# Two output projections and one input projection issued as pairs of 512 and 256 columns

## The chip, the cores and the metric

The kernel runs on one core of a Trainium2 chip. Its time is the device time of one execution in microseconds (us). Times below are of single executions; the median is over the runs named.

## The reference

One sequence of T = 256 tokens of width D = 2048 in float32 goes through two transformer-like layers. Cut to what matters here:

```python
# layer 1
h = rms_norm(x, mix_norm)
proj = h @ w_in                       # mixers and gates
merged = sigmoid(g_a)*(y_a @ wb_a) + sigmoid(g_b)*(y_b @ wb_b) + sigmoid(g_c)*(y_c @ wb_c)
x = x + merged @ w_out                # output projection of layer 1
x = x + conv_ffn(rms_norm(x, ffn_norm), w_up, conv_w, conv_b, w_down)
x = rms_norm(x, final_norm)
# layer 2
h = rms_norm_2(x, g_mix)
proj = h @ w_in_2                     # second input projection: latents, rope key, q, k, v, gates
x = x + (g0 * y_a + g1 * y_b) @ w_o_2 # output projection of layer 2
gt, up = split(rms_norm_2(x, g_ffn) @ w_gate_up)
x = x + (silu(gt) * up) @ w_down_2
```

## The kernel before

**Layout.** Activations are kept transposed: a tile has 128 features on the partitions and 256 tokens along the row, and KT = 16 such tiles make a width of 2048. xT is the residual stream, hT the normalised input, and a large arena holds all else. Weights stream from HBM in units: one unit (2048 columns, 1 MB) holds the 16 weight tiles of 128 x 128 that make one output tile. They land in a ring of RING = 4 slots, issued by the SyncE queue as soon as `consumed[s]` says that TensorE is done with the slot.

**High and low halves.** Large projections run in float32r with both operands split: ScalarE rounds a unit to w_high (line 1029), VectorE makes w_low = w - w_high (the helper at line 1459) in place in the ring, AHEAD = 2 units before they are used. Activations are split in the same way. A product of two numbers is high x high + high x low + low x high.

**Two ways to issue it.** `project_split` has three matmuls of 256 columns for each weight tile, all into one half of a bank: w_high with the high activations, w_high with the low ones, w_low with the high ones. `project_pairs` has two: w_high with the high and low activations side by side, 512 columns into both halves of the bank (high sum in half 0, low sum in half 1), and w_low with the high activations, 256 columns into half 0. Whoever drains the bank must then add its halves. Before the change the up projections use `project_pairs` and the down projections the same pattern (`acts_both`, whose high and low tiles lie 44 tiles apart); the output projections and the second input projection use `project_split`.

**Banks.** Unit n of a projection writes bank s = n mod 4; `drained[s]` says when it may be written again. Banks 4 to 7 serve the normalisations and the down projections.

**Output projections** (`merged_out`, once in each layer, 16 units): the drain is in `residual_raw` on VectorE, which adds the bank to xT[:, n]; ScalarE then rounds the new tile with its gain and squares it (`round_raw`), VectorE makes its low part (`lower_raw`) and adds up the squares (`sum_raw`). When the 16 units are done, `drained_all` makes TensorE wait for every drain, and the up projection follows on the raw residual tiles (`ups`: 8 of them in hT as up_early, 8 in the arena as up_late).

**Second input projection.** Its feature-major part has IN2 = 26 units: the first by `raw_unit`, one more, then two and four rounds of four. The input is the raw residual of layer 1 (`in2_high`, `in2_low`: 8 tiles in hT, 8 in the arena, high and low side by side in each), and the norms are put on as a factor when the bank is drained: `P2[:, u] = bank * xrs`. xrs is ready only after a chain that starts behind the first unit: a matmul of ones sums the squares, VectorE and ScalarE take two reciprocal roots with steps of refinement, and units of weights are rounded and lowered in between. After the 26 units come the units that produce tokens on the partitions (`tokens`), which wait for the drains of two banks.

In VectorE's code `link` makes an instruction's successor wait for it, and `tt` is a tensor-tensor operation; nearly all of VectorE's rows have line 1459, that of `tt`. All matmuls have line 486.

Of the kernel before, what the change touches and what calls it, by code (L numbers as in the profile page):

```python
# [36 lines left out]
P = 128  # L37
T = 256
TB = T // P
D = 2048  # L40
KT = D // P
# [139 lines left out]
def build(nc, t, out):  # L181

    with ExitStack() as ctx:
        def sb(name, shape, dt=F32):
            return ctx.enter_context(nc.sbuf_tensor(name, shape, dt))

        def alias(name, base, shape, at=0):

            return nc.alloc_sbuf_tensor_at(name, shape, R32, offset=base + at * T * 4)
# [3 lines left out]
        xT = sb("xT", [P, KT, T])  # L193
# [15 lines left out]
        xrs = sb("xrs", [P, T])  # L209
        xtmp = sb("xtmp", [P, T])  # L210
        ARENA = nc.sbuf_bytes_remaining // 4 // 16 * 16
        arena = sb("arena", [P, ARENA])
        arena_base = nc.sbuf_base - ARENA * 4

        def tiles(at, n):
            assert at + n * T <= ARENA, (at + n * T, ARENA)
            return arena[:, at:at + n * T].rearrange("p (k t) -> p k t", t=T)
# [9 lines left out]
        in2 = [part[:, k] for part, n in ((in2_early, 8), (in2_mid, 3), (in2_next, 1), (in2_late, KT - LATE))  # L227
               for k in range(n)]
        in2_high, in2_low = [x[:, 0] for x in in2], [x[:, 1] for x in in2]
        out_high, out_low = (alias(f"out_{n}", arena_base, [P, KT, T], a) for n, a in (("high", 28), ("low", 46)))  # L230
        out2_high, out2_low = (alias(f"out2_{n}", arena_base, [P, KT, T], a) for n, a in (("high", 18), ("low", 34)))
        y_high, y_low = alias("y_high", arena_base, [P, 12, T], 4), alias("y_low", arena_base, [P, M_TILES, T], 0)
        u_high = alias("u_high", hT_base, [P, S5_TILES, T])
        y2_high, y2_low = alias("y2_high", arena_base, [P, KT, T], 66), alias("y2_low", arena_base, [P, 26, T], 0)
# [38 lines left out]
        P2 = tiles(0, 26)  # L273
# [14 lines left out]
        bank = [ctx.enter_context(nc.psum_tensor(f"bank{i}", [P, 2, T], F32)) for i in range(8)]  # L288
        bank_row = [b[:].rearrange("p a t -> p (a t)") for b in bank]

        def sem(name):
            return ctx.enter_context(nc.semaphore(name))
# [5 lines left out]
        drained = [sem(f"bank_drained{s}") for s in range(RING)]  # L298
# [9 lines left out]
        norm_mean, norm_rooted, norm_done = sem("norm_mean"), sem("norm_rooted"), sem("norm_done")  # L308
# [169 lines left out]
        def _(pe):  # L478
            units = Units(landed, rounded, lowered, consumed, drained)
# [3 lines left out]
            norm = [0]  # L483
# [17 lines left out]
            def unit_split(body, bank_used=True):  # L501
                s, _, _, _, free = units.next(split=True)
                pe.wait_ge(lowered[s], units.lowered[s].value())
                if bank_used and (not isinstance(free, int) or free > 0):
                    pe.wait_ge(drained[s], free)
                body(s).then_inc(consumed[s], 1)
# [8 lines left out]
            def rounds_split(n, body):  # L515
                with pe.Fori(0, n) as i:
                    units.enter(i, split=1)
                    for j in range(RING):
                        unit_split(body)
                units.leave(n)  # L520

            def mm3(o, s, c, high, low, first, last):

                c = slice(c * P, (c + 1) * P)
                mm(o, w_high[:, s, c], high, first, False)
                mm(o, w_high[:, s, c], low, False, False)
                return mm(o, w_low[:, s, c], high, False, last)

            def each(x):
                return [x[:, k] for k in range(KT)]  # L530
# [13 lines left out]
            def project_split(high, low, waits=None, at=0):  # L544
                def body(s):
                    for k in range(KT):
                        if waits:
                            waits(k)
                        last = mm3(bank[at + s][:, 0], s, k, high[k], low[k], k == 0, k == KT - 1)
                    return last  # L550
                return body

            merges = [0]

            def merged_out(high, low):

                n = merges[0]
                merges[0] += 1

                def waits(k):  # L560
                    pe.wait_ge(merged_lowered, KT * n + k + 1)
                unit_split(project_split(high, low, waits))
                for j in range(3):
                    unit_split(project_split(high, low))
                rounds_split(3, project_split(high, low))

            def project(s):
                for k in range(KT):
                    last = mm(bank[s][:, 0], ring[:, s, k * P:(k + 1) * P], hT[:, k], k == 0, k == KT - 1)
                return last  # L570
# [19 lines left out]
            def drained_all():  # L590
                for s, n in units.all_drained():
                    pe.wait_ge(s, n)
# [3 lines left out]
            def raw_unit(project, second=False):  # L596

                n = raws[0]
                raws[0] += 1

                def waits(k):
                    pe.wait_ge(raw_lowered, KT * n + k + 1)
                unit_split(project(waits))
                pe.wait_ge(raw_summed, (KT - 1) * raws[0])
                mm(bank[4][:, 0], ones[:], xms[:]).then_inc(norm_summed, 1)
                norm[0] += 1
                if second:
                    pe.wait_ge(raw_summed2, KT - 1)
                    mm(bank[5][:, 0], ones[:], sum2).then_inc(norm_summed, 1)
                    norm[0] += 1  # L610
# [99 lines left out]
            for part in range(2):  # L710
                s = take()
# [92 lines left out]
            for f in range(S5_TILES):  # L804
                if f % 2 == 0:
                    s = take()
# [15 lines left out]
            s = take()  # L822
# [10 lines left out]
            s = take()  # L833
# [24 lines left out]
            for j in range(3):  # L858
                unit_split(branches(False))
            rounds_split(3, branches(False))  # L860
            merged_out(each(out_high), each(out_low))
            drained_all()
            raw_unit(lambda waits: project_pairs(ups, waits))
            for j in range(3):
# [2 lines left out]
            down(0)  # L867
            for b in range(2):
                pe.wait_ge(down_drained[b], 1 + KT // 2)
            raw_unit(lambda waits: project_split(in2_high, in2_low, waits), second=True)  # L870
            unit_split(project_split(in2_high, in2_low))
            rounds_split(2, project_split(in2_high, in2_low))
            banks_back()
            rows_back()
            turn_factor()
            rounds_split(4, project_split(in2_high, in2_low))
            tokens(False, in2_high, in2_low)
            sum_squares()
            tokens(True, in2_high, in2_low)
# [100 lines left out]
            for j in range(3):  # L980
                unit_split(branches2(False))
            rounds_split(3, branches2(False))
            merged_out(each(out2_high), each(out2_low))
            drained_all()
            raw_unit(lambda waits: project_pairs(ups, waits))
            for j in range(3):
# [456 lines left out]
        def _(dve):  # L1443
            V = nc.vector
            units = Units(landed, rounded, lowered, consumed, drained)
            chain = Count(dve_chain)
            norm = [0]
            M, ADD, SUB, MAX, MIN = ALU.mult, ALU.add, ALU.subtract, ALU.max, ALU.min

            def link(ins):  # L1450
                ins.then_inc(dve_chain, 1)
                chain.add()
                dve.wait_ge(dve_chain, chain.value())
# [4 lines left out]
            def tt(o, a, b, op=M):  # L1458
                return V.tensor_tensor(o, a, b, op)  # L1459
# [195 lines left out]
            for u in range(MIX):  # L1655
# [24 lines left out]
                if u >= MIX - KT:  # L1680
                    k = u - (MIX - KT)
# [165 lines left out]
            s, _, _, there, _ = units.next(False)  # L1847
# [68 lines left out]
            def residual_raw(gain):  # L1916

                for n in range(KT):
                    s, _, _, there, free = units.next()
                    lower_weights(UNIT)  # L1920
                    dve.wait_ge(consumed[s], there)
                    tt(xT[:, n], xT[:, n], bank[s][:, 0], ADD).then_inc(drained[s], 1)
                    if n:
                        lower_raw(n - 1, ups[n - 1][:, 0], ups[n - 1][:, 1], v(gain, n - 1))
                        sum_raw(n - 1)
                    if n == KT - 1:
                        dve.wait_ge(drained[s], free + 1)
                lower_raw(KT - 1, ups[KT - 1][:, 0], ups[KT - 1][:, 1], v(gain, KT - 1))
                sum_raw(KT - 1)
                raws[0] += 1  # L1930
# [65 lines left out]
            pairs, convs, acts = Count(silu_pair), Count(conv_made), Count(acts_rounded)  # L1996
# [91 lines left out]
            refine(xms[:], xrs[:], xtmp[:], to=mix2_rs)  # L2088
            link(tt(xrs[:], final_rs, mix2_rs))
            V.tensor_copy(xtmp[:, 0:1], xrs[:, 0:1]).then_inc(norm_done, 1)  # L2090


            IN2 = 26
            for u in range(IN2):
                while ahead.pos - base < min(IN2, max(u + AHEAD + 1, 5)):
                    lower_weights(UNIT)
                s, _, _, there, _ = units.next()
                dve.wait_ge(consumed[s], there)
                tt(P2[:, u], bank[s][:, 0], xrs[:]).then_inc(drained[s], 1)
                if 6 <= u < 6 + KT:  # L2100
                    k = u - 6
                    stt(xT[:, k], xT[:, k], v("final_norm", k), final_rs).then_inc(x_normed, 1)
# [45 lines left out]
            for half in range(2):  # L2148
                for g in range(2):
                    k = 2 * half + g  # L2150
# [13 lines left out]
            for h in range(2 * HEADS):  # L2164
                e, m = ES[h % 2], small[:, h % 2]
                s = bank[4 + h % 2]
# [225 lines left out]
```

## Time and profile before

| | |
|---|---|
| median of 3 runs | 3117.86 us (3116.12 to 3118.37) |
| the profiled execution | 3121.36 us |
| its span, first to last instruction | 3119.6 us, mean granted TensorE clock 0.994 |
| TensorE matmul busy | 3083.7 us, 99%, 18712 matmuls |
| TensorE weight loads busy | 2746.7 us, 88% |
| VectorE busy | 1812.5 us, 58% |
| ScalarE busy | 1202.8 us, 39% |
| GpSimd busy | 101.8 us, 3% |
| DMA | 530.23 MB, mean 170 GB/s |

The profile comes from one execution. Matmuls overlap in the array, so the duration of one (0.28 us for 256 columns, 0.39 for 512) is not the distance from one to the next; that distance is read from start times, or from a stretch divided by its number of matmuls. A mean granted clock of 1.00 in a stretch is 2.4 GHz, 0.50 is 1.2 GHz.

### The profile page before, as it was taken

What the parts mean: (1) busy time and instruction counts of PE and PEld (TensorE: products, weight loads), DVE (VectorE), ACT (ScalarE), POOL (GpSimd) and SP (SyncE); (2) the same over time, 40 slices, a digit from 0 to 9 for tenths busy, and PEclk for the clock granted to TensorE, in tenths of its full rate; (3) what the DMA queues carried; (4) which work ended last, traced back from release to release, by engine and by line L of the source; (5) the groups of instructions that cost most, each with busy time, mean ns of one, the idle gap of its engine ahead of it and who ended that gap; (6) DMA issues with size and microseconds to landing.
All of it is one profiled execution on the core that took longest, in us unless ns stands there. A gap on an engine that the chain in (4) does not pass through costs nothing.

```text
span 3119.6 us, 47133 instructions
## 1 busy us (share of the span) xinstructions
PE 3083.7 (99%) x18712; PEld 2746.7 (88%) x18712; DVE 1812.5 (58%) x2356; ACT 1202.8 (39%) x1351; POOL 101.8 (3%) x80
## 2 busy tenths in 40 slices
PE   8999999999999999999999999999999999999999
PEld 8898898889998888888889977788999888888888
DVE  6673352867678888875555333322566666665444
ACT  5453102114444444444443312244445444444333
POOL 0000000000000000000000310000000000000000
PEclk9999999999999999999999999899999999999999
DMA  6554332445555555555555543223455555555555
GB/s 225 185 187 155 108 121 95 159 152 188 183 183 190 192 193 190 188 174 192 187 194 183 183 164 108 81 95 123 162 187 189 188 188 189 190 193 172 192 186 183
DMA packets 80147, 530.23 MB, mean 170 GB/s; under 512 B 9152, under 2 KB 9536, under 8 KB 27712
## 3 DMA queue, kind: packets, MB, share of 16 engines
q1 hardware_dynamic: 80064, 529.07, 49.3%
q8 instruction: 59, 0.97, 0.1%
q14 instruction: 24, 0.20, 0.0%
HBM read 526.94 MB, written 2.10 MB: 170 GB/s over the span
## 4 chain that ended last, share of the span: by engine, by line
PE 97%; DVE 1%; ACT 1%; issue 0%; DMA 0%; SPq 0%; ACTq 0%; DVEq 0%
PE bank L486 97%; DVE w_low L1459 0%; ACT w_high L1029 0%; DVE arena L1459 0%; PE bank L963 0%; DVE arena L1456 0%; DMA xT<-in_xT 0%; DVE arena L1489 0%; DVE xrs L1489 0%; DVE acts_both L1459 0%; DVE xtmp L1459 0%; ACT arena L1114 0%; ACT mix_high L1133 0%; DVE xT L1459 0%; ACT L1152 0%
## 5 line engine op out<-in xcount | busy, mean ns | idle before, releaser
L1459 DVE TENSOR_TENSOR w_low<-ring,w_high 128x2048 fp32r<-128x2048 f32 (+1 forms) x440 | 922.8, 2098 | 434.6 <-ACT w_high L1029 430.8
L1029 ACT ACTIVATE w_high<-ring 128x2048 fp32r<-128x2048 f32 (+1 forms) x448 | 787.1, 1758 | 468.6 <-DMA ring<-in_w_down 232.2
L486 PE MATMUL bank<-hT,ring 128*128 128x256 f32 x2560 | 571.7, 384 | 1.2 <-ACT arena L1376 1.2
L486 PEld LDWEIGHTS bank<-hT,ring 128*128 128x128 f32 x2560 | 489.8, 192 | 76.8 <-issue 7.7
L486 PE MATMUL bank<-up_late,w_high 128*128 128x512 f32 x1408 | 496.9, 392 | 0.0
L486 PE MATMUL bank<-up_early,w_high 128*128 128x512 f32 x1408 | 490.6, 390 | 1.3 <-issue 0.8
L486 PE MATMUL bank<-acts_both,w_high 128*128 128x512 f32 x1408 | 488.5, 392 | 1.5 <-DVE arena L1459 1.3
L486 PE MATMUL bank<-acts_both,w_low 128*128 128x256 f32 x1408 | 393.5, 280 | 0.0
L486 PE MATMUL bank<-up_late,w_low 128*128 128x256 f32 x1408 | 393.4, 279 | 0.0
L486 PE MATMUL bank<-up_early,w_low 128*128 128x256 f32 x1408 | 389.8, 277 | 0.0
L486 PEld LDWEIGHTS bank<-acts_both,w_high 128*128 128x128 f32 x1408 | 264.3, 188 | 58.7 <-issue 1.6
L486 PEld LDWEIGHTS bank<-up_early,w_high 128*128 128x128 f32 x1408 | 264.3, 188 | 58.1 <-issue 0.9
L486 PEld LDWEIGHTS bank<-up_late,w_high 128*128 128x128 f32 x1408 | 264.2, 188 | 57.8
L486 PEld LDWEIGHTS bank<-acts_both,w_low 128*128 128x128 f32 x1408 | 267.3, 190 | 0.0
L486 PEld LDWEIGHTS bank<-up_late,w_low 128*128 128x128 f32 x1408 | 266.8, 189 | 0.0
L486 PEld LDWEIGHTS bank<-up_early,w_low 128*128 128x128 f32 x1408 | 264.3, 188 | 0.1
L1300 ACT ACTIVATE xms<-bank 128x256 f32<-128x256 f32 x176 | 67.9, 386 | 453.5 <-PE bank L486 446.0
L1459 DVE TENSOR_TENSOR arena<-arena 128x256 f32<-128x256 f32 (+6 forms) x283 | 202.3, 721 | 29.7 <-DVE arena L1459 8.2
L486 PE MATMUL bank<-mix_high,w_high 128*128 128x256 f32 x544 | 154.5, 284 | 13.6 <-DVE w_low L1459 13.6
L486 PE MATMUL bank<-mix_high,w_low 128*128 128x256 f32 x544 | 154.2, 284 | 0.0
L486 PE MATMUL bank<-mix_low,w_high 128*128 128x256 f32 x544 | 153.8, 283 | 0.0
L486 PE MATMUL bank<-y_low,w_high 128*128 128x256 f32 x512 | 144.5, 282 | 0.0
(277 smaller groups left out, 4016.2 us busy)
## 6 DMA issues: line engine op xcount, KB each, us to landing
ring<-in_w_up SPq DMA_DIRECT2D x176, 1024.0 KB, 4.8
ring<-in_w_down SPq DMA_DIRECT2D x128, 704.0 KB, 4.0
ring<-in_w_in SPq DMA_DIRECT2D x66, 1024.0 KB, 4.8
ring<-in_w_mix SPq DMA_DIRECT2D x62, 1024.0 KB, 4.9
ring<-in_w_gates SPq DMA_DIRECT2D x48, 1024.0 KB, 4.9
ring<-in_w_branch SPq DMA_DIRECT2D x16, 1024.0 KB, 4.8
ring<-in_w_out SPq DMA_DIRECT2D x16, 1024.0 KB, 4.8
ring<-in_w_o SPq DMA_DIRECT2D x16, 1024.0 KB, 4.8
```

The lines of the kernel that those rows point to most:

```text
L486: return nc.tensor.matmul(o, lhsT, rhs, start=first, stop=last)
L1029: A(w_high[:, s, 0:cols], ring[:, s, 0:cols], ACT.Copy).then_inc(rounded[s], 1)
L1300: A(xms[:], bank[s][:, 1], ACT.Copy).then_inc(half_copied, 1)
L1459: return V.tensor_tensor(o, a, b, op)
```

## The change

The 16 units of each output projection and the 26 feature units of the second input projection are issued by `project_pairs` in place of `project_split`. The high and low activations of the output projections become one tensor each (`out_both`, `out2_both`) over the same places in the arena. The drains add the two halves: `residual_raw` adds half 0 and half 1 to xT one after the other, linked; the drain of the input projection multiplies both halves by xrs, gives the bank back, waits for its own semaphore and adds the second product. Ahead of these drains VectorE waits once for the copy that ends the norm's chain, since xtmp, which that copy writes, now takes the second products.

```diff
-        out_high, out_low = (alias(f"out_{n}", arena_base, [P, KT, T], a) for n, a in (("high", 28), ("low", 46)))
-        out2_high, out2_low = (alias(f"out2_{n}", arena_base, [P, KT, T], a) for n, a in (("high", 18), ("low", 34)))
+        out_both = alias("out_both", arena_base, [P, 2, KT + 2, T], 28)
+        out2_both = alias("out2_both", arena_base, [P, 2, KT, T], 18)
+        out_high, out_low, out2_high, out2_low = out_both[:, 0], out_both[:, 1], out2_both[:, 0], out2_both[:, 1]
...
-            def merged_out(high, low):
+            def merged_out(both):
...
-                unit_split(project_split(high, low, waits))
+                pairs = [both[:, :, k] for k in range(KT)]
+                unit_split(project_pairs(pairs, waits))
                 for j in range(3):
-                    unit_split(project_split(high, low))
-                rounds_split(3, project_split(high, low))
+                    unit_split(project_pairs(pairs))
+                rounds_split(3, project_pairs(pairs))
...
-            raw_unit(lambda waits: project_split(in2_high, in2_low, waits), second=True)
-            unit_split(project_split(in2_high, in2_low))
-            rounds_split(2, project_split(in2_high, in2_low))
+            raw_unit(lambda waits: project_pairs(in2, waits), second=True)
+            unit_split(project_pairs(in2))
+            rounds_split(2, project_pairs(in2))
             banks_back()
             rows_back()
             turn_factor()
-            rounds_split(4, project_split(in2_high, in2_low))
+            rounds_split(4, project_pairs(in2))
...
                     dve.wait_ge(consumed[s], there)
-                    tt(xT[:, n], xT[:, n], bank[s][:, 0], ADD).then_inc(drained[s], 1)
+                    link(tt(xT[:, n], xT[:, n], bank[s][:, 0], ADD))
+                    tt(xT[:, n], xT[:, n], bank[s][:, 1], ADD).then_inc(drained[s], 1)
...
             V.tensor_copy(xtmp[:, 0:1], xrs[:, 0:1]).then_inc(norm_done, 1)
+            dve.wait_ge(norm_done, norm[0])
...
                 dve.wait_ge(consumed[s], there)
-                tt(P2[:, u], bank[s][:, 0], xrs[:]).then_inc(drained[s], 1)
+                tt(P2[:, u], bank[s][:, 0], xrs[:])
+                tt(xtmp[:], bank[s][:, 1], xrs[:]).then_inc(drained[s], 1)
+                dve.wait_ge(drained[s], units.drained[s].value())
+                link(tt(P2[:, u], P2[:, u], xtmp[:], ADD))
```

## Rows read from the trace of the kernel before

**Rows 1.** The page: busy time of the engines, and the chain that ended last, by engine.

```profile
PE 3083.7 (99%) x18712; PEld 2746.7 (88%) x18712; DVE 1812.5 (58%) x2356; ACT 1202.8 (39%) x1351; POOL 101.8 (3%) x80
...
PE 97%; DVE 1%; ACT 1%; issue 0%; DMA 0%; SPq 0%; ACTq 0%; DVEq 0%
```

**Rows 2.** Stretches: busy us (matmuls) by engine, granted clock, DMA share, GB/s.

```profile
810.00:885.00 75.00, 75.00 (x639) 75.00 (x638) 45.58 (x55) 35.53 (x42) 0.00 (x0) 1.00 0.55 184
1654.00:1767.00 113.00, 113.00 (x959) 112.85 (x958) 57.67 (x54) 36.64 (x20) 3.96 (x1) 1.00 0.54 186
900.00:1370.00 470.00, 470.00 (x2729) 414.65 (x2728) 406.82 (x561) 218.67 (x250) 30.13 (x34) 1.00 0.55 188
2873.00:3116.00 243.00, 243.00 (x1404) 214.78 (x1403) 116.13 (x94) 86.24 (x64) 0.00 (x0) 1.00 0.55 188
```

**Rows 3.** The timeline of TensorE inside the up projection: start us, us, what.

```profile
1101.67 0.39 PE L486 MATMUL bank<-up_early,w_high 128*128 128x512 f32 x1
...
1102.01 0.39 PE L486 MATMUL bank<-up_early,w_high 128*128 128x512 f32 x1
...
1102.70 0.39 PE L486 MATMUL bank<-up_late,w_high 128*128 128x512 f32 x1
...
1103.05 0.39 PE L486 MATMUL bank<-up_late,w_high 128*128 128x512 f32 x1
```

**Rows 4.** Groups of matmuls: xcount, then busy us, mean ns, idle before.

```profile
L486 PE MATMUL bank<-out_high,w_low 128*128 128x256 f32 x512 | 144.4, 282 | 0.0
...
L486 PE MATMUL bank<-in_early,w_low 128*128 128x256 f32 x208 | 58.9, 283 | 0.0
```

**Rows 5.** The chain of waits in order of time: start us, us, what.

```profile
888.82 0.77 issue
...
1772.95 0.56 issue
...
2384.44 0.43 DVE xT L1459
```

**Rows 6.** The timeline of VectorE, an xT sum of either kind.

```profile
888.86 0.42 DVE L1459 TENSOR_TENSOR xT<-xT,bank 128x256 f32<-128x256 f32 x1 [0.25 <-PE bank L486]
...
1604.73 0.88 DVE L1459 TENSOR_TENSOR xT<-xT,bank 128x256 f32<-128x256 f32 x2 [0.44 <-PE bank L486]
```

**Rows 7.** The timeline of VectorE at the head of the second input projection.

```profile
1628.82 0.42 DVE L2076 TENSOR_SCALAR xms<-bank 128x256 f32<-128x256 f32 x1 [1.09 <-PE bank L486]
...
1646.96 0.15 DVE L2090 COPY xtmp<-xrs 128x1 f32<-128x1 f32 x1
1647.03 1.08 DVE L1459 TENSOR_TENSOR arena<-bank,xrs 128x256 f32<-128x256 f32 x3
1648.02 2.28 DVE L1459 TENSOR_TENSOR w_low<-ring,w_high 128x2048 fp32r<-128x2048 f32 x1
1650.22 0.42 DVE L1459 TENSOR_TENSOR arena<-bank,xrs 128x256 f32<-128x256 f32 x1
1650.56 2.28 DVE L1459 TENSOR_TENSOR w_low<-ring,w_high 128x2048 fp32r<-128x2048 f32 x1
```

**Rows 8.** The timeline of TensorE there, in brackets what ended its idle time.

```profile
1645.91 0.28 PE L486 MATMUL bank<-in_late,w_low 128*128 128x256 f32 x1
1647.59 0.48 PE L486 MATMUL bank<-in_early,w_high 128*128 128x256 f32 x2 [1.40 <-DVE arena L1459]
```

**Rows 9.** Stretches around stops of TensorE, columns as in rows 2.

```profile
1619.70:1622.40 2.70, 0.25 (x2) 0.00 (x0) 2.61 (x3) 0.02 (x1) 0.00 (x0) 1.00 0.72 209
1992.80:1996.00 3.20, 0.36 (x2) 0.00 (x0) 2.72 (x4) 0.00 (x0) 0.00 (x0) 0.60 0.32 133
1996.00:2014.00 18.00, 17.94 (x37) 10.93 (x38) 2.50 (x7) 3.59 (x6) 0.00 (x0) 0.50 0.00 1
2198.00:2200.80 2.80, 0.40 (x4) 0.16 (x2) 0.50 (x1) 2.76 (x3) 0.00 (x0) 1.00 0.62 173
2200.80:2206.00 5.20, 5.19 (x27) 5.03 (x28) 3.60 (x3) 3.87 (x4) 0.00 (x0) 0.67 0.27 112
```

More of the change, by code:

```diff
@@ L860, in _ @@
             rounds_split(3, branches(False))
-            merged_out(each(out_high), each(out_low))
+            merged_out(out_both)
             drained_all()
@@ L982, in _ @@
             rounds_split(3, branches2(False))
-            merged_out(each(out2_high), each(out2_low))
+            merged_out(out2_both)
             drained_all()
```

## Prediction

> **What bounds the kernel now.** I read the page's busy times and its chain of waits first. TensorE is busy for 99% of the span and the chain runs through its matmuls for 97% [rows 1], so a change counts by what it does to the matmul stream and to the few places where TensorE stands still. Then I read the stages as stretches, to see whether the matmuls that are replaced run at a pace of their own or wait for something. In the first layer's output projection TensorE is busy for all of 75.00 us, as it is in the input projection of layer two and in the up and down projections [rows 2]. The reader is to see that no stage named in the change waits for weights, DMA or VectorE; what differs between them is the time per matmul. Last I read the seams: where TensorE waits for a bank to be drained, since the drain is what the change makes longer.
>
> **The price of the two schemes.** The old form issues three matmuls of 256 columns for one tile of 128 weights, the new one a matmul of 512 and one of 256: both stream 768 columns, so only what each matmul costs beside its columns can be saved. Old form: 639 matmuls in 75.00 us are 117.4 ns each and 959 in 113.00 us are 117.8 [rows 2]. Counted over a unit (16 tiles, 48 matmuls) that is 5.63 to 5.66 us; I take 5.65. New form, by a stage that already uses it with every operand in the arena: the down projection has 1404 matmuls in 243.00 us [rows 2], 173.1 ns each, and 32 of them are 5.54 us; since some matmul records at the edges are missing I take 5.55. The up projection, with half of its moving tiles in hT and half in the arena: 2729 in 470.00 us, 172.2 ns, 5.51 us a unit [rows 2]. The matmuls themselves show where that comes from: a pair from up_early (in hT) is followed by the next after 0.34 us, a pair from up_late (in the arena) after 0.35 [rows 3].
>
> **Output projections: two times 16 units.** The count agrees with 512 matmuls of out_high with low weights [rows 4]. Both out_both and out2_both lie wholly in the arena, high and low halves apart, as acts_both does, so the down projection is the nearest row: 32 x (5.65 - 5.55) = 3.2 us gained. Bounds: nothing, if the pairs stream no better there, and 32 x 0.21 = 6.8 us if every pair ran at up_early's 0.34 us (16 x 0.34 = 5.44 a unit). I take 3.2, because every pair from the arena that I see runs at 0.35.
>
> **Input projection of layer two: 26 units.** in_early's 208 matmuls with low weights are 8 tiles of each of 26 units [rows 4]; those 8 lie in hT and the other 8 in the arena, the up projection's mixture. That gives 5.65 - 5.51 = 0.14 us a unit. But the first four units gain nothing by themselves: they fill the four banks, and the fifth waits for the first drain, which waits for the norm factor. TensorE stops after a matmul at 1645.91 and goes on at 1647.59 [rows 8], released by VectorE. So 22 x 0.14 = 3.1 us.
>
> **What that first drain costs.** The factor's chain begins when the matmul of ones behind the first unit is read, at 1628.82 [rows 7], and that comes 0.14 us earlier. From there the chain is VectorE and ScalarE work that the edit leaves alone, up to the copy at 1646.96. Then the edit adds a wait for this copy (it began 0.07 us before the first product; waiting for its 0.15 us and a semaphore gives about 0.12 more) and a second product before the bank is given back: three products take 1.08 us together, so one more is 0.33 [rows 7]. 0.12 + 0.33 - 0.14 = 0.3 us later than before. I add 0.3.
>
> **What queues behind it on VectorE.** Each drain is now two products, a wait for its own semaphore and a linked sum: 0.33 + 0.42 + 0.04 + 0.42 + 0.04 = 1.25 us in place of 0.33. Three of them stand in front of the weights' low part for the sixth unit. They begin at about 1647.0 and end at 1650.8, that low part (2.28 us [rows 7]) ends at 1653.1, and TensorE, back at 1647.9, wants it at 1653.4. So it is hidden with 0.3 us to spare; if the cover is gone it costs some tenths. Later units give VectorE 2.28 + 1.25 and one operation more of about 0.42, 4.0 us of work in 5.51.
>
> **The seams.** Before each up projection TensorE waits for all banks: 0.77 us after the last output unit in layer one, and behind the last xT sum of 0.43 in layer two [rows 5]. One sum takes 0.42 and two linked ones 0.88 [rows 6], so each seam grows by 0.46: 0.92 us for both. The input projection ends in the same way, the token stage waiting 0.56 us for the last product [rows 5]; a second product adds 0.33. ScalarE gets each xT tile 0.46 us later too, and then rounds it, squares it and rounds weights that are wanted a whole unit later. No DMA is added or moved; a weight slot comes free at most 0.14 us sooner per unit, as in the up projection, which streams at 188 GB/s without a wait [rows 2].
>
> **Sum.** -3.2 - 3.1 + 0.3 + 0.92 + 0.33 = -4.75, say -4.7 us. On the profiled execution's 3121.36 us (span 3119.6) that is 3116.7. The runs' median of 3117.86 lies 3.5 us under that execution, so I put the same difference on it: 3113.2 us, 0.15% less.
>
> The page "TensorE: Matmul & The Clock Gate" of the Trainium skill (section "Wait — 56ns, not 53.3ns?") speaks against it: a warm matmul costs its columns at 2.4 GHz and about 2.5 ns more, whatever its size. An estimate by that page: 54 units x 16 fewer matmuls x 2.5 ns = 2.2 us, and with the costs above the change would bring 0.6 us. The trace does not agree, with 11 ns a matmul above the columns.
>
> **The rivals.**
> A: the pairs bring little or nothing in the new places; something else than the count of matmuls (the order in which w_high and w_low alternate, say) made the up and down projections faster. For it: these projections differ from the changed stages in everything else as well. Against it: two stages with different operands both have it. With no gain at all the costs stay: +1.6 us, 3119.4. The page of the Trainium skill named above is a half-way form of it. 14%.
> B: the 0.35 us is not a matter of the arena, and the output projections get up_early's pace: 6.8 in place of 3.2, and the same for the other half of the input tiles (22 x 0.07 = 1.5) at the most; -8.3 us with the first alone, 3109.5. Against it: the down projection, all arena, shows 0.35 throughout. 14%.
> C: the stop before the fifth unit grows from 1.6 us to 2.5 (it begins 0.6 earlier and ends 0.3 later), and the granted clock falls there from 2.4 to 1.2 GHz. After 2.8 us without matmuls at 2198 the next 5.2 us ran at a mean of 0.67, while after as long a stop at 1619.7 the clock stayed at 1.00 [rows 9]. A short stretch like the first costs (1 - 0.67) x 5.2 = 1.7 us: -3.0, 3114.9. 10%.
> D, the other side: the same stop is followed by a long stretch at 1.2 GHz, as the 3.2 us at 1992.8 were by 18 us at 0.50 [rows 9], now in a stage that TensorE bounds. That loses half of some 20 us, 10 us: +5.5, 3123.4, and it makes the kernel slower as soon as the stretch is longer than 9.4 us. Against it: the stop stays shorter than the one at 1992.8, and the matmuls behind it are dense. 4%.
> E: VectorE falls behind at the head of the input projection, if a drain costs 0.1 us more than I put; some tenths, in the main case's range.
>
> **How the numbers follow.** The likeliest case (58%) is the sum: 3113.2, by itself 3111.5 to 3115. Moving from a gain of nothing to B's needs 3109.5 to 3119.4; leaving out most of D and the far ends of A and B gives 3109.4 to 3119.0. About 0.2% (6.2 us) is what a measurement of this kernel can tell from no change. Faster by more than that: B and the lower tail of the main case, 0.23. Slower by more: D, with something for a wait that I have not seen, 0.06. Within: 0.71.
>
> **What would show it.** In the changed profile, right steps look like this: a unit interval of 5.55 us in the output projections (drains of xT 5.55 apart, not 5.65) and 5.51 in the input projection; 16 matmuls fewer in each of 58 units, 928 in all; the seams before the up projections 0.46 us wider; the fifth input unit starting about 2.5 us after the fourth ends, at clock 1.00, and none between it and the sixth. Wrong would be a unit of 5.65 or of 5.44 us in the output projection, a stretch at half clock behind 1647, or TensorE waiting for w_low in the input projection. The half-clock stretches between 1900 and 2210 lie outside the change but may fall otherwise when all before them is 3 us earlier; the three runs' spread of 2.3 us is my measure for that.

## The result and the profile after

The changed kernel took 3130.86 us (median of 6 runs, 3128.07 to 3131.28), the kernel before 3118.18 (median of 6). The ratio is 1.0031, 95% interval 1.0021 to 1.0041: about 0.3% slower, where 0.15% faster was forecast and 3119.0 was the upper end of the range. (The ratio is not the quotient of the two medians, which is 1.0041.) The profiled execution has a span of 3129.5 us, 9.9 more than the profiled one before; both lie above their kernels' medians, which are 12.7 us apart. The account below is one of the 9.9 us.

The page of the changed kernel first, busy times and then the chain by engine, against [rows 1]; under it stretches inside the output and the input projection, and three stretches at half clock, with the columns of [rows 2]:

```profile
PE 3083.2 (99%) x17784; PEld 2707.9 (87%) x17784; DVE 1845.2 (59%) x2440; ACT 1202.7 (38%) x1351; POOL 101.4 (3%) x80
...
PE 91%; DVE 5%; ACT 3%; issue 1%; DMA 0%; SPq 0%; ACTq 0%; DVEq 0%
```

```profile
810.00:885.00 75.00, 75.00 (x434) 66.29 (x434) 48.45 (x64) 34.21 (x39) 0.00 (x0) 1.00 0.56 195
1660.00:1772.00 112.00, 112.00 (x652) 98.67 (x651) 75.54 (x96) 36.73 (x20) 4.22 (x1) 1.00 0.55 187
889.10:895.90 6.80, 3.89 (x12) 3.35 (x13) 5.55 (x8) 3.90 (x4) 0.00 (x0) 0.50 0.21 88
1653.70:1657.10 3.40, 3.40 (x11) 2.92 (x12) 3.23 (x8) 0.68 (x1) 0.00 (x0) 0.50 0.59 246
2391.00:2397.70 6.70, 5.39 (x17) 4.63 (x18) 4.98 (x8) 3.90 (x4) 0.00 (x0) 0.50 0.14 60
```

The matmuls did what the change says: 928 fewer, 172.8 ns each in the output projection (5.53 us a unit), 171.8 in the input projection (5.50). But the chain that ended last, 97% TensorE before, has 8% of VectorE and ScalarE in it now. A stretch of that chain in the first output projection, and its end ("issue" is time in which the engine waited for nothing that the profile shows):

```profile
840.64 1.82 ACT w_high L1031
842.48 2.29 DVE w_low L1461
845.59 0.51 ACT up_early L1082
846.41 1.81 ACT w_high L1031
...
886.35 5.66 issue
```

It goes round: round a unit's weights, make their low part, (drain a bank), round the new tile, round the next unit's weights, 5.77 us a turn (846.41 - 840.64). And it ends in TensorE standing still until 892.01. TensorE's first matmul behind the seam, in both layers:

```profile
892.01 0.77 PE L487 MATMUL bank<-up_early,w_high 128*128 128x512 f32 x1 [5.76 <-issue]
```

```profile
2392.31 0.80 PE L487 MATMUL bank<-up_early,w_high 128*128 128x512 f32 x1 [4.71 <-DVE xT L1461]
```

Where the 9.9 us are, from the start of each stage's first matmul to the next one's (the seam: from the start of the last output matmul to the start of the first up matmul), in us; "forecast" is what my terms gave:

| stretch | before | after | difference | forecast |
|---|---|---|---|---|
| all ahead of the first output projection | 798.21 | 797.33 | -0.87 | 0 |
| output projection's matmuls, each layer | 90.34 | 88.64 | -1.70, twice | -1.6, twice |
| seam to the up projection, layer 1 | 1.05 | 6.04 | +4.99 | +0.46 |
| seam to the up projection, layer 2 | 0.80 | 4.98 | +4.18 | +0.46 |
| up projection, layer 1 | 485.69 | 487.52 | +1.83 | 0 |
| up projection, layer 2 | 487.27 | 489.77 | +2.50 | 0 |
| second input projection, to the token stage | 151.06 | 151.77 | +0.71 | -2.5 |

The rest is within 0.1 us. The sum is +9.9. The first row is untouched code: a stretch of 6.8 us at half clock fell there before, one of 3.4 us after.

### The profile page after: what moved, and what is told of

Its sections match the earlier page's. It is cut to its first block, busy times and chain, and to the rows that moved or that the text cites. A ratio compares the mean times of both kernels' runs of the same rounds, so it can differ in the third digit from the quotient of the medians.

```text
span 3129.5 us, 45372 instructions
## 1 busy us (share of the span) xinstructions
PE 3083.2 (99%) x17784; PEld 2707.9 (87%) x17784; DVE 1845.2 (59%) x2440; ACT 1202.7 (38%) x1351; POOL 101.4 (3%) x80
## 4 chain that ended last, share of the span: by engine, by line
PE 91%; DVE 5%; ACT 3%; issue 1%; DMA 0%; SPq 0%; ACTq 0%; DVEq 0%
PE bank L487 91%; DVE w_low L1461 3%; ACT w_high L1031 2%; DVE xT L1461 1%; DVE arena L1461 0%; ACT up_early L1082 0%; ACT up_late L1082 0%; PE bank L965 0%; DVE arena L1458 0%; ACT xrs L1073 0%; ACT xtmp L1073 0%; DMA xT<-in_xT 0%; DVE arena L1491 0%; DVE xrs L1491 0%; DVE xtmp L1461 0%
## 5 line engine op out<-in xcount | busy, mean ns | idle before, releaser
L487 PE MATMUL bank<-out_both,w_high 128*128 128x512 f32 x512 | 177.6, 392 | 0.0
```

What stands on the lines that cost most here:

```text
L487: return nc.tensor.matmul(o, lhsT, rhs, start=first, stop=last)
```

## The experiments

The theory drawn from this trace: the output projection has a closed loop beside TensorE. On VectorE the code puts the low weights of unit n+2 ahead of the drain of unit n; they wait for ScalarE's w_high of the same unit; ScalarE makes that only after it has rounded and squared tile n-1, and for this it waits for the drain of unit n-1. A turn took 5.31 us before and the second sum (0.46) makes it 5.77, past TensorE. The rivals: the pairs themselves cost in their new places; the half-clock stretches fell by chance; the input projection is at fault. Ten kernels ran, in three groups (e1 to e4, e5 to e8, e9 and e10), each group with runs of the kernel before on the same chip (medians 3121.61, 3121.32 and 3119.12 us).

**e1, a slower drain without pairs.**

```diff
-                    tt(xT[:, n], xT[:, n], bank[s][:, 0], ADD).then_inc(drained[s], 1)
+                    link(stt(xT[:, n], bank[s][:, 0], 0.5, xT[:, n], M, ADD))
+                    stt(xT[:, n], bank[s][:, 0], 0.5, xT[:, n], M, ADD).then_inc(drained[s], 1)
```

> The kernel before, matmuls untouched; only each drain of an output projection is drawn out: the same sum is added to xT in two linked steps of half the bank each (about 0.5 us more VectorE work per unit, the sums' value unchanged). Loop theory (VectorE drain, ScalarE rounding and squaring of the new tile, ScalarE w_high, VectorE w_low, next drain form a closed loop of 5.31 us that the change lengthened to 5.77, past TensorE's 5.53 to 5.65 a unit): drains 5.85 us apart instead of 5.65, TensorE standing 4 to 6 us before each up projection, a stretch at half clock behind it; 9 to 13 us slower than before, 3127 to 3131. Matmul theory (pairs into two bank halves cost more in their new places): nothing here, within 1 us of before but for the seams (about +1). Clock theory (half-clock stretches that fall by chance): at most +2.

Measured: 3132.82 us (5 runs), ratio 1.0039, interval 1.0025 to 1.0053. VectorE's timeline, with no wait for TensorE ahead of a drain, and TensorE's stops at the two seams:

```profile
884.59 0.88 DVE L1456 SCALAR_TENSOR_TENSOR xT<-bank,xT 128x256 f32<-128x256 f32 x2
...
888.15 2.29 DVE L1459 TENSOR_TENSOR w_low<-ring,w_high 128x2048 fp32r<-128x2048 f32 x1 [1.96 <-ACT w_high L1029]
890.36 0.88 DVE L1456 SCALAR_TENSOR_TENSOR xT<-bank,xT 128x256 f32<-128x256 f32 x2
```

```profile
891.55 0.77 PE L486 MATMUL bank<-up_early,w_high 128*128 128x512 f32 x1 [4.19 <-issue]
...
2391.34 0.51 PE L486 MATMUL bank<-up_early,w_high 128*128 128x512 f32 x1 [3.14 <-DVE xT L1456]
```

The drains are 5.77 us apart (not the 5.85 expected: this operation took no longer than a plain sum), TensorE stands for 4.2 us at the first seam and the clock falls behind it; at the second it stands for 3.1 us and the clock stays at 1.00. The median is above the 3127 to 3131 expected. The trace is that of the fastest of the five runs (3128.15), 6.8 us over the span of before: +3.4 and +2.6 at the seams, +1.6 for the half-clock stretch in the first up projection, less 1.5 ahead of the edit. With every matmul as before, the drain alone brings a loss of the same kind and size: the rival of the matmuls is out. What the slower runs of e1 have on top is not shown.

**e2, the changed kernel, draining first.**

```diff
                     s, _, _, there, free = units.next()
-                    lower_weights(UNIT)
                     dve.wait_ge(consumed[s], there)
                     link(tt(xT[:, n], xT[:, n], bank[s][:, 0], ADD))
...
                         sum_raw(n - 1)
+                    lower_weights(UNIT)
```

> The changed kernel with one order turned round in the output projections' drain: VectorE drains unit n first and makes the low weights of unit n+2 after it, so the loop is open. Loop theory: drains 5.53 us apart, the stop before each up projection 1.4 us in place of 6.0 and 5.0, no half-clock stretch behind it; 10 to 13 us faster than the changed kernel, 3117 to 3121 (3113 to 3117 if the input projection's half-clock stretches stay away as well). Matmul theory: the loss is in the matmuls and stays, 3129 to 3132. Clock theory: the stretches would fall anyway, at most 4 us back.

Measured: 3115.64 us (11 runs), ratio 0.9984, interval 0.9975 to 0.9993. VectorE's timeline:

```profile
880.55 0.88 DVE L1461 TENSOR_TENSOR xT<-xT,bank 128x256 f32<-128x256 f32 x2 [1.74 <-PE bank L487]
...
882.08 2.28 DVE L1461 TENSOR_TENSOR w_low<-ring,w_high 128x2048 fp32r<-128x2048 f32 x1
886.10 0.87 DVE L1461 TENSOR_TENSOR xT<-xT,bank 128x256 f32<-128x256 f32 x2 [1.74 <-PE bank L487]
```

The same operations with the same durations, in another order: now VectorE waits 1.74 us for TensorE in each unit, drains are 5.55 apart, the seams are 1.50 and 1.24 us, and the up projections take 485.69 and 487.23 us, as before. The loss was in the order. And the half-clock stretches at the seams go with the long stops: they stand at the stops of 5.76, 4.71 and 4.19 us (five of five, in the changed kernel, e1 and e3), and at none of the seams with a stop of 2.03 us or less; e1's 3.14 us had none.

**e3 and e4, one half of the change each.** e3 has the output projections in pairs alone, e4 the input projection alone; each undoes the other's lines of the diff. Cut to the calls, against the changed kernel:

```diff
 # e3
-            raw_unit(lambda waits: project_pairs(in2, waits), second=True)
+            raw_unit(lambda waits: project_split(in2_high, in2_low, waits), second=True)
 # e4
-                unit_split(project_pairs(pairs, waits))
+                unit_split(project_split(high, low, waits))
```

> Only the two output projections in pairs; the second input projection as before. Loop theory: carries the whole loss, 9 to 11 us over before, 3127 to 3130. Matmul theory with the input projection at fault: no loss here. The rival that the input projection's head (longer stop, half clock) is the main cause: at most +3.

> Only the second input projection in pairs; the output projections as before. By my prediction's terms -2.5 us when the clock stays up (22 units at 0.15 us less, 0.3 and 0.33 given back): 3115 to 3116; with half-clock stretches at its head, 1.6 us each as the changed kernel's trace has two, +0.7: 3119. Loop theory: no more than that, since this drain has no ScalarE rounding behind it. The rival that this part is at fault: 3124 or more.

Measured: e3 3130.82 us (4 runs), ratio 1.0039 (1.0023 to 1.0054), with the seams of the changed kernel, 6.04 and 4.99 us. e4 3122.31 us (10 runs), ratio 1.0000 (0.9991 to 1.0009); four of its executions lie at 3117 us with a mean granted clock of 0.995 and six at 3121.3 to 3124.5 with 0.993 or 0.992, and the profiled one is of the latter, with two stretches at half clock at the head of the input projection. So the output projections carry the loss. That the input projection gains where the clock stays up is not shown by e4: its fastest executions (3117.08) do not lie under the fastest of before (3116.13). The nearest comparison is that of e8 and e10 below.

**e5, the loop cut on ScalarE instead**, in the changed kernel:

```diff
                     A(ups[n][:, 0], xT[:, n], ACT.Copy, scale=v(gain, n)).then_inc(raw_rounded, 1)
+                    if n < KT - 1:
+                        round_weights(UNIT)
                     square_raw(n)
```

(and the call at the head of the loop's body moved ahead of the loop).

> The changed kernel with one order turned round on ScalarE: in the output projections it rounds the next unit's weights before it squares the new xT tile, which takes 0.3 us out of the loop and nothing else. Loop theory: 5.77 - 0.30 = 5.47 us, below TensorE's 5.54, so drains 5.54 apart, the stop before each up projection near 1.5 us as in e2, and 8 to 12 us faster than the changed kernel. Rival (it is VectorE alone that cannot keep up, by its own work of 2.29 + 0.87 + 0.48 + 0.42 us a unit): ScalarE's order changes nothing, 3129 to 3132.

Measured: 3116.18 us (10 runs), ratio 0.9990 (0.9981 to 1.0000). The seams are 1.51 and 1.25 us. Drains in the first layer:

```profile
836.51 0.87 DVE L1463 TENSOR_TENSOR xT<-xT,bank 128x256 f32<-128x256 f32 x2
...
841.98 0.87 DVE L1463 TENSOR_TENSOR xT<-xT,bank 128x256 f32<-128x256 f32 x2
```

The square weighs 0.3 us in the chain, has nothing to do with VectorE, and taking it out of the loop brings all of the loss back: it is the loop, not VectorE's own work. The turn is the one expected, too: the first drain of the layer is 0.9 us late, the next eleven follow at 5.46 to 5.47 us and so catch up with TensorE, and from there on they stand 5.55 apart, TensorE's own pace.

**e6, a drain lengthened to just below TensorE's pace**, in the kernel before:

```diff
-                    tt(xT[:, n], xT[:, n], bank[s][:, 0], ADD).then_inc(drained[s], 1)
+                    link(tt(xT[:, n], xT[:, n], bank[s][:, 0], ADD))
+                    V.tensor_scalar(xT[:, n], xT[:, n], 1.0, None, M).then_inc(drained[s], 1)
```

> The kernel before with a smaller delay in the drain of the output projections than e1: the bank is added as before, and a linked VectorE product by 1.0 (about 0.33 us) stands behind it ahead of the release. Loop theory: 5.31 + 0.33 = 5.64 us, just below the 5.65 of TensorE's three matmuls, so no lag builds up: drains stay 5.65 apart, each seam 0.33 us wider, +0.7 us in all. Rival (any work added to the drain costs in proportion, e1 having cost some 9 us for 0.5 us a unit): +5 to +7 us.

Measured: 3124.34 us (10 runs), ratio 1.0020 (1.0011 to 1.0029), more than expected. The trace has the output projections at 90.34 us as before and the up projections at 485.75 and 487.60, so nothing builds up. But the first seam is 2.31 us, not 1.38. The first drain of layer 1 begins 0.8 us behind its unit's last matmul; before, with a loop of 5.31, that was made up at 0.34 us a unit, and the loop of 5.64 here makes up 0.01. In both layers the loop has one longer turn, 5.97 us (6.10 in the changed kernel and in e1), where ScalarE's square waits for VectorE's first sum of squares; so the second seam is 1.28 and not 1.13, though its first drain is on time. The larger part is in the input projection, +1.4 us with a stretch at half clock at 1622, in code that it doesn't touch. Neither theory had the number; the proportional one fails on the seams. The same trace shows how much room the loop had: 0.33 us more in each turn still kept TensorE's pace.

**e7 to e10, the clock at the head of the input projection.** The traces so far show a pattern. TensorE stands idle ahead of the fifth input unit, as in [rows 8]; the changed kernel, e2, e4 and e5 each have this row (here of the changed kernel):

```profile
1653.55 0.66 PE L487 MATMUL bank<-in_early,w_high 128*128 128x512 f32 x1 [2.21 <-DVE xtmp L1461]
```

and in each a stretch of 3.4 us at half clock stands behind the stop (1653.7, 1646.7, 1649.9 and 1646.4). With 1.40 us idle, before and in e1, e3 and e6, there is none. These are single traces, one for each kernel. e7 is e2 with this in the norm factor's chain on VectorE:

```diff
             V.tensor_scalar(xms[:], bank[4][:, 0], 1.0 / D, EPS, M, ADD).then_inc(norm_mean, 1)
-            lower_weights(UNIT)
             dve.wait_ge(norm_rooted, norm[0])
             refine(xms[:], xrs[:], xtmp[:], to=final_rs)
```

(That unit's low part is made up later, by the loop ahead of the first drain of this stage.)

> e2 (drain first) with one order more turned round, at the head of the second input projection: VectorE no longer makes a unit's low weights between the first mean and the first refinement of the norm factor, so its chain no longer waits for ScalarE's rounding there. If the longer stop ahead of the fifth unit (2.5 us) is what lets the clock fall (it fell in three traces of three with the input projection in pairs, in none of three without): no stop there, no half-clock stretch, 146 us from the first input unit to the token stage in place of 150.3; 3.5 to 4.5 us faster than e2, a ratio of 0.997 to before. If the clock falls by chance alone, only the 2.5 us. If the factor's chain is not what holds the first drain: as e2.

Measured: 3114.74 us (11 runs), ratio 0.9977 (0.9968 to 0.9986). There is no stop ahead of the fifth unit and no stretch behind it. From the first input unit to the token stage it took 147.76 us, 2.5 less than e2 (150.29), not the 4.3 expected, because a stretch stood at the stage's start this time, at the end of the stop between the down projection and it (the profiled execution is the fastest of the eleven, 3109.35):

```profile
1617.70:1621.10 3.40, 3.29 (x10) 2.84 (x11) 1.48 (x5) 3.34 (x5) 0.00 (x0) 0.50 0.57 239
```

e8 has this last edit alone, on the kernel before.

> The kernel before with that second order alone, all three projections still in threes of 256 columns: what of e7 belongs to the order and not to the pairs. Only the stop of 1.56 us can go, the clock did not fall there: 1.5 us faster, 149.5 us from the first input unit to the token stage in place of 151.06, within 0.1% of before. If more comes back, the factor's chain held more than the stop that the trace shows.

e8: 3118.78 us (10 runs), ratio 0.9999 (0.9990 to 1.0009), 149.42 us for the stage: 1.64 less, as expected.

e9 draws the stop out, on the kernel before:

```diff
             link(tt(xrs[:], final_rs, mix2_rs))
+            for _ in range(2):
+                link(V.tensor_scalar(xrs[:], xrs[:], 1.0, None, M))
```

> The kernel before (all in threes) with the stop ahead of the fifth input unit drawn out from 1.56 to about 2.2 us: two linked VectorE products by 1.0 (0.33 us each) at the end of the norm factor's chain. If it is the length of the stop that lets the clock fall, a half-clock stretch now stands behind 1647 in this trace too, as in the four traces with pairs in the input projection (stops of 2.2 to 2.5 us): +0.7 for the stop and about +1.6 for the clock from the first input unit to the token stage, 153.4 us in place of 151.06. If the stretch belongs to the pairs: +0.7 alone, 151.7, clock 1.00 there.

e9: 3122.43 us (10 runs), ratio 1.0006 (0.9996 to 1.0015). TensorE's row and a stretch behind it:

```profile
1646.26 0.47 PE L486 MATMUL bank<-in_early,w_high 128*128 128x256 f32 x2 [2.06 <-DVE arena L1459]
```

```profile
1647.00:1650.00 3.00, 3.00 (x19) 3.00 (x18) 3.00 (x3) 0.89 (x1) 0.00 (x0) 0.61 0.49 205
```

The clock fell there in this kernel of threes too, once its stop was 2.06 us and not 1.40: pairs are not needed for it. The profiled execution is the slowest of the ten (3126.85), and the interval of the ratio includes 1, so this shows that the clock can fall there, not how often it does. The stage took 154.78 us and not 153.4, because the clock fell at its start as well.

e10 is e7 with the last down bank drained before the next low weights are made:

```diff
+                        last_unit = n == KT - 1 and q == 3
+                        if not last_unit:
+                            lower_weights(DOWN * P if 4 * n + q + AHEAD < 4 * KT else UNIT)
-                        lower_weights(DOWN * P if 4 * n + q + AHEAD < 4 * KT else UNIT)
...
                     tt(xT[:, n], xT[:, n], bank[4 + b][:, 1], ADD).then_inc(down_drained[b], 1)
+                    if last_unit:
+                        lower_weights(UNIT)
```

> e7 with the same turn at a third place: at the end of the first down projection VectorE drains the last bank before it makes the low weights of the second input unit (2.29 us, which stood ahead of that drain and held TensorE for 2.7 us). The stop there should be about 1.2 us, and the half-clock stretch that stood at this seam in e7 (1617.7) and in the changed kernel (1626.4) should stay away: 1.5 us of stop and, in the executions that had the stretch, 1.5 us more; 1.5 to 3 us faster than e7, a ratio near 0.9970 to before. If the last drain is not what holds TensorE there: as e7.

Measured: 3109.25 us (9 runs), ratio 0.9973 (0.9963 to 0.9983). The stop at the stage's start is 1.02 us, the stage takes 146.22, and the down projection's stretch 245.69 in place of 247.17. No half-clock stretch stands in the stage. In threes, with the same order in the norm factor's chain and no such stretch either, it took 149.42 (e8), so pairs bring about 3.2 us there when the clock stays up. e10 has the lowest median of all, about 0.27% below the kernel before; e7, in another group, had 0.23%, and the two intervals overlap.

## Why the prediction was wrong

**The matmuls: right.** 5.53 and 5.50 us a unit against 5.55 and 5.51 forecast; -1.70 us twice against -1.6 twice. Rival A (pairs bring nothing) and rival B (the pace of hT in the arena) are both out. The floor of 2.5 ns a matmul that the Trainium skill gives in "TensorE: Matmul & The Clock Gate", section "Wait — 56ns, not 53.3ns?", does not price this case: a removed matmul saved 1.70 us / 256 = 6.6 ns in the output projections.

**The seams: the step that failed.** It was "each seam grows by 0.46: 0.92 us for both", with the sentence on ScalarE, which "rounds weights that are wanted a whole unit later". True of TensorE, which wants them a unit later; but VectorE wants them at once, since it makes their low part ahead of the next drain. I asked who waits for the drain and not whether the drain waits, by way of three others, for itself. The seams took 9.2 us more instead of 0.92. In layer 1 the first drain began 0.93 us behind its unit's last matmul and the last one 4.58: 14 turns of 5.77 us against TensorE's 5.55, 0.22 each, and the long one of 6.10. Before, the last drain began 0.04 behind. With the 0.46 itself that makes 5.0 us, against 4.99 measured; in layer 2, from 0.13 to 3.78, it makes 4.2 against 4.18. e1 (the loop without pairs), e2 and e5 (the pairs without the closed loop, opened at two places) show it.

The trace of before had it in sight. The first drains of the stage stood 5.31 us apart, faster than TensorE's units, which is the loop's own pace while it catches up:

```profile
804.85 0.41 DVE L1459 TENSOR_TENSOR xT<-xT,bank 128x256 f32<-128x256 f32 x1
...
810.16 0.41 DVE L1459 TENSOR_TENSOR xT<-xT,bank 128x256 f32<-128x256 f32 x1
```

Against a unit of 5.65 us that is a room of 0.34 a turn (e6 put 0.33 into it and still kept pace), and against the new unit of 5.55 one of 0.24; 0.46 went into it. VectorE's wait of just 0.25 us for TensorE ahead of that sum [rows 6] was the hint of how small the room was. I used that row for the sum's duration and left its bracket unread. So "no stage named in the change waits for weights, DMA or VectorE" was a right reading of the time before and no ground for the time after.

**The clock behind the seams: not foreseen there.** Rival C had the mechanism and about the size, at another place. Stops of 5.76 and 4.71 us each brought 6.8 us at half clock, part of it within the stop; the rest cost 1.83 and 2.50 us in the up projections. With the stops gone (e2) both are back to 485.7 and 487.2. The Trainium skill's page "TensorE: Matmul & The Clock Gate", section "HAM oscillation — how this bites in real kernels", warns that a wait between bursts of matmuls can bring the low clock back at each burst; both seams of this trace agree, with 6.8 us at 0.50 from within each stop on. The second seam of e1, 3.14 us at a clock of 1.00, shows that not every such wait does it.

**The input projection: the terms right, rival C true as well.** Without half-clock stretches the terms give -2.5 us. The trace has +0.71 with two stretches, one at each of the two stops; e2, with one, has -0.77. The difference of 1.5 to 1.7 us for each is C's price. So C, which I gave 10%, came true beside the main case: the longer stop had its stretch in four traces of four. These are single traces; how often it has one over many executions is not shown.

**VectorE at the head (E)** kept up: TensorE had no other stop in that stage. D, the long stretch, did not come.

**Together:** -4.7 forecast; +8.3 for the seams, +4.3 for the clock behind them, +3.2 for the clock in the input projection (what is left of its 0.71 when the terms' -2.5 is taken off), -0.9 ahead of the change and -0.2 on the matmuls make +10.0, against 9.9 in the spans. What stays open: e6's ratio of 1.0020 would be 6.2 us, while its median is 3.0 us and its trace 2.7 us over before; the trace has 1.7 us of its own edit and the rest in half-clock stretches elsewhere. Such stretches also move a kernel's executions by some us without any edit (the kernel before ran from 3116.16 to 3125.67 us in its 33 runs beside e5 to e8, at mean clocks of 0.996 to 0.993), so a gain of 0.1% needs the stages' times and not the total.

## What to carry to other kernels

Before an operation is added to a drain, follow what waits for it until you are back at the drain: if in-order engines close a loop there, its turn must stay below the bottleneck's unit. The room left is the unit less the turn (5.65 - 5.31 = 0.34 us here, and less once the change makes the unit shorter), with a short wait for the bottleneck in brackets before the drain as its sign (0.25 us); it is not the engine's idle share (VectorE was at 58%). Such a loop is opened by order alone: drain first, prepare the next unit after it. And a stop of the matmul engine costs more than its length when the clock falls behind it, so small stops are worth removing too: e10, which has the fewest, has the lowest median.

## What the runs showed of the hardware

A pair of 512 and 256 columns with its moving tile in hT follows the last after 0.34 us, one with the tile in the arena after 0.35 [rows 3], in the stages changed here as well (5.50 against 5.53 us a unit); the runs do not say why. Ahead of the fifth input unit, in dense matmul work, the granted clock fell to 1.2 GHz behind stops of 2.06 and 2.21 us (five traces of five: the changed kernel, e2, e4, e5, e9) and not behind 1.40 (four of four). At the seams before the up projections, also in dense work, it fell at stops of 4.19 to 5.76 us (five of five: the changed kernel, e1, e3) but stayed at 2.4 GHz behind 3.14 us (e1, second seam) and 2.03 us (e6, first seam). Behind 2.42 to 2.64 us at the start of the second input projection it fell in six traces (the changed kernel, e3, e4, e6, e7, e9) and not in five (before, e1, e2, e5, e8). So the length of a stop alone does not decide it, and what does is not shown.
